# High and low columns side by side, and 512-column products in the first, q, k, v and widening stages

## What is computed

```python
h = rms_norm(x, attn_norm_g)
q, k, v, p = split(h @ w_in)            # 4 x 1024 columns
q, k = rms_norm(heads(q)), rms_norm(heads(k))
a = moba_attention(q, k, v, rel_bias)   # 8 heads of 128, one block of 256 keys, causal
m = multiscale_pool(p, pool_w, pool_scale)
x = x + concat(a, m) @ w_out            # "mix"
x = x + conv_ffn(rms_norm(x), w_up, conv_w, conv_b, w_down)   # "up" to 2 x 5632, "down"
```

## Time and profile before

| what | value |
|---|---|
| median of 3 runs | 2434.01 us (2433.1 to 2434.31) |
| the profiled execution | 2437.58 us |
| its span, first to last instruction | 2435.8 us |
| PE matmul busy | 2407.7 us, 99% |
| VectorE, ScalarE, GpSimd busy | 73%, 48%, 24% |
| mean granted TensorE clock | 0.998 |

### The profile page before, as it was taken

How to read it: one execution, slowest core, us unless ns; L and a number is a source line. 1 busy time by engine, 2 the same in 40 slices (tenths; PEclk the granted TensorE clock), 3 DMA queues, 4 the chain that set the end, 5 groups by cost and what they waited for, 6 DMA issues and landing times.

```text
span 2435.8 us, 53642 instructions
## 1 busy us (share of the span) xinstructions
PE 2407.7 (99%) x18808; PEld 2321.6 (95%) x18808; DVE 1769.6 (73%) x3095; ACT 1162.7 (48%) x1647; POOL 578.4 (24%) x402
## 2 busy tenths in 40 slices
PE   8999999999999999999999999999999999999998
PEld 8999899999999988898999999999999999999987
DVE  6877877777777755578888878888882566666665
ACT  5444444444444444447566643333544444444443
POOL 0400000000000000005242447777777300100100
PEclk9999999999999999999999999999999999999999
DMA  7554555555555666666555555555555555555544
GB/s 272 193 172 145 187 185 187 177 188 189 181 186 185 207 186 189 186 216 198 179 169 172 170 166 177 172 175 194 171 175 173 184 168 163 162 164 175 157 162 140
DMA packets 152398, 438.21 MB, mean 180 GB/s; under 512 B 32324, under 2 KB 47213, under 8 KB 152189
## 3 DMA queue, kind: packets, MB, share of 16 engines
q1 hardware_dynamic: 148844, 424.68, 53.5%
q0 software_dynamic: 3184, 12.14, 1.8%
q10 hardware_dynamic: 288, 0.30, 0.0%
HBM read 434.88 MB, written 11.09 MB: 183 GB/s over the span
## 4 chain that ended last, share of the span: by engine, by line
PE 95%; DVE 2%; DMA 1%; ACT 1%; issue 1%; DVEq 0%; SPq 0%; POOL 0%; ACTq 0%
PE bank L1121 24%; PE bank L1122 24%; PE bank L1123 24%; PE bank L1115 11%; PE bank L1116 6%; PE bank L1355 1%; DVE wlo L1569 1%; PE bank L1475 1%; PE bank L1326 1%; PE bank L1465 1%; PE bank L1455 1%; PE bank L1118 0%; DMA raw<-w_qkv 0%; PE bank L1482 0%; ACT whi L627 0%
## 5 line engine op out<-in xcount | busy, mean ns | idle before, releaser
L1121 PE MATMUL bank<-xhl,whi 128*128 128x256 f32 (+1 forms) x4494 | 1285.6, 286 | 4.9 <-DVE wlo L1569 3.9
L1123 PE MATMUL bank<-xhl,wlo 128*128 128x256 f32 (+1 forms) x4494 | 1278.3, 284 | 0.0
L1122 PE MATMUL bank<-xhl,whi 128*128 128x256 f32 (+1 forms) x4494 | 1277.6, 284 | 0.0
L627 ACT CAST whi<-raw 128x1024 fp32r<-128x1024 f32 x784 | 810.8, 1044 | 574.5 <-PE bank L1123 431.5
L1569 DVE TENSOR_TENSOR wlo<-raw,whi 128x1024 fp32r<-128x1024 f32 x624 | 765.8, 1238 | 263.4 <-ACT whi L627 259.2
L1121 PEld LDWEIGHTS bank<-xhl,whi 128*128 128x128 f32 x4494 | 849.8, 189 | 8.0 <-DVE wlo L1569 4.2
L1123 PEld LDWEIGHTS bank<-xhl,wlo 128*128 128x128 f32 x4494 | 848.9, 189 | 0.0
L1122 PEld LDWEIGHTS bank<-xhl,whi 128*128 128x128 f32 x4494 | 845.5, 188 | 0.8 <-issue 0.2
L568 POOL TENSOR_TENSOR wlo<-raw,whi 128x1024 fp32r<-128x1024 f32 x160 | 379.2, 2378 | 128.0 <-ACT whi L627 128.0
L1115 PE MATMUL bank<-fhl,whi 128*128 128x512 f32 x928 | 329.1, 398 | 0.0
L1116 PE MATMUL bank<-fhl,wlo 128*128 128x256 f32 x960 | 264.3, 281 | 0.0
(11 more groups left out here) (283 smaller groups left out, 2436.5 us busy)
## 6 DMA issues: line engine op xcount, KB each, us to landing
raw<-w_up SPq DMA_DIRECT2D x176, 512.0 KB, 3.9
raw<-w_na SPq DMA_DIRECT2D x128, 512.0 KB, 3.7
raw<-w_ssm SPq DMA_DIRECT2D x96, 512.0 KB, 3.9
raw<-w_glu SPq DMA_DIRECT2D x96, 512.0 KB, 3.5
raw<-w_down SPq DMA_DIRECT2D x80, 512.0 KB, 3.8
raw<-w_qkv SPq DMA_DIRECT2D x48, 512.0 KB, 3.8
raw<-w_mix SPq DMA_DIRECT2D x32, 512.0 KB, 3.7
raw<-w_outa SPq DMA_DIRECT2D x32, 512.0 KB, 3.6
```

Of the source, the lines that this page charges most:

```text
L627: A.copy(whi[s][:, :], raw[s][:, :]).then_inc(sem("hi_done"), 1)
L1121: T.matmul(to_, wh, xh_, start=head, stop=False)
L1122: T.matmul(to_, wh, xl_, start=False, stop=False)
L1123: ins = T.matmul(to_, wl, xh_, start=False, stop=last)
```

## The change

**Layout.** `xh` and `xl` share one row of 544 columns for each K-tile (`XW`), `fh`/`fl` and `oh`/`ol` rows of 512: the 256 high columns that a product reads end where the 256 low ones begin. **Products.** pin, qkv and up join the stages with two matmuls for a K-tile, and in all of these the 512 columns are now one run. **Evacuation.** In pin, qkv and up, ScalarE first copies the bank's upper half to `lows` (an area of `sq`), then VectorE adds it to the lower half and multiplies by the norm, in two dependent instructions instead of one. **Order.** In `up` the third split is moved ahead of the first taps on VectorE, and the gate and the tap on ScalarE behind casts.

```diff
+        XW = 2 * TOK
+        xh, xl = xhl[:, 0:KT * XW], xhl[:, TOK:KT * XW]
...
+        fh, fl = fhl[:, 0:2 * FT * SEQ], fhl[:, SEQ:2 * FT * SEQ]
...
+        lows = sq[:, 0:SEQ]
...
+            def lower(phase, i, j, k):
+
+                wait_chunk_done(act, phase, i, j)
+                act.wait_ge(sem("bank_free"), tile(phase, i, k) + 2)
+                A.copy(lows[:, :], pbank(phase, k)[:, SEQ:2 * SEQ]).then_inc(sem("low_out"), 1)
...
             def qkv(i, before=True, pooled=False):
                 for j in range(12):
                     split("qkv", i, j)
                     m, jj = divmod(j, 6)
                     attn = before or m
+                    if jj % 2:
+                        lower("qkv", i, j, j // 2)
                     if jj == 2 and attn:
                         probs(i * 2 + m)
...
+                split("up", i, 1)
+                if lead:
+                    act.wait_ge(sem("acc_done"), 2 + 32)
+                lower("up", i, 1, 0)
+                split("up", i, 2)
+                tap(0)
+                split("up", i, 3)
...
+                gate(nt[:, 0:SEQ], cg[:, :], ACT.Silu, "eg_up")
+                lower("up", i, 3, 1)
+                tap(1)
...
-                    if wide and phase in ("mix", "down", "naout"):
-                        both = pb_[:, 0:2 * n].rearrange("p (t n) -> p t n", t=2)
+                    if wide and phase in ("pin", "qkv", "mix", "up", "down", "naout"):
                         if not last:
-                            T.matmul(both, wh, halves(mh, ml, o, n), start=head, stop=False)
+                            T.matmul(pb_[:, 0:2 * n], wh, mh[:, o:o + 2 * n], start=head, stop=False)
                         ins = T.matmul(out, wl, mh[:, o:o + n], start=False, stop=False)
...
+            def scaled_halves(phase, i, k, out, r):
+
+                dve.wait_ge(sem("low_out"), low_tile(phase, i, k) + 1)
+                ch.link(V.tensor_tensor(out, pbank(phase, k)[:, 0:SEQ], lows[:, :], ADD))
+                freed(phase, i, k, V.tensor_tensor(out, out, r, MUL))
...
                 split("up", i, 1)
-                scaled("up", i, 1, 0, ug[:, 2:SEQ + 2], rs[1], SEQ, META)
+                scaled_halves("up", i, 0, ug[:, 2:SEQ + 2], rs[1][:, META:TOK])
+                split("up", i, 2)
                 taps(ug, cg, 0, i).then_inc(sem("cg_ready"), 1)
-                split("up", i, 2)
                 split("up", i, 3)
-                scaled("up", i, 3, 1, uv[:, 2:SEQ + 2], rs[1], SEQ, META)
+                scaled_halves("up", i, 1, uv[:, 2:SEQ + 2], rs[1][:, META:TOK])
```

More of the change, by code:

```diff
@@ L155, in program @@
         cv = at("cv", SEQ, F32, U + 3136)
[L157 to L158 removed]
+        a = Y + 2 * 16 * SEQ * 4
+        b = a + 28 * SEQ * 4
         praw = at("praw", 8 * TOK, F32, a)
@@ L270, in tile, with low_tile @@
             return i * PHASES[phase][2] + (first(phase, 2) + k)
+        def low_tile(phase, i, k):
+            return tile(phase, i, k) - (16 if phase == "up" else 0)
         def pbank(phase, k):
@@ L766, in qkv @@
                         pool_hi(2 * m + jj // 4)
+            lower_pin(0)
+            lower_pin(1)
             split("pin", 1, 2)
+            lower_pin(2)
             split("pin", 1, 3)
-            with act.Fori(2, 4) as i:
+            lower_pin(3)
+            for i in range(2, 4):
                 for j in range(4):
                     split("pin", i, j)
+                    if j % 2:
+                        lower_pin(2 * i + j // 2)
             ch.begin()
@@ L805, in up, with tap @@
             def up(i, lead=0, last=False):
[L806 to L820 removed]
+                def tap(k):
+                    u, c = ((ug, cg), (uv, cv))[k]
+                    evacuated("up", i, k)
+                    A.activation(c[:, :], u[:, 0:SEQ], ACT.Identity,
+                                 bias=vcol("ffn_conv", 4 * k + 3, i, 8),
+                                 scale=vcol("ffn_conv", 4 * k, i, 8)).then_inc(sem("tap_done"), 1)
+                if not lead:
+                    split("up", i, 0)
+                split("up", i, 1)
[5 more added lines that the diff above has]
+                split("up", i, 3)
+                if last:
+                    split("down", 0, 0)
+                act.wait_ge(sem("cg_ready"), i + 1)
+                gate(nt[:, 0:SEQ], cg[:, :], ACT.Silu, "eg_up")
+                lower("up", i, 3, 1)
+                tap(1)
             up(0, 1)
@@ L1243, in mixing @@
             def mixing(n, part, kts, out=None, start=False, stop=False, done=True):
-                product("mix", part, n, n % 2, fh, fl, kts, SEQ, 0, SEQ, start, stop, out, done)
+                product("mix", part, n, n % 2, fh, fl, kts, 2 * SEQ, 0, SEQ, start, stop, out, done)
             pe.wait_ge(sem("pool_free"), 4)
@@ L1508, in projecting @@
             def projecting(n, n_tile, kts, start=False, stop=False, done=True):
-                product("naout", n // 4, n % 4, n_tile % 2, oh, ol, kts, SEQ, 0, SEQ, start, stop,
+                product("naout", n // 4, n % 4, n_tile % 2, oh, ol, kts, 2 * SEQ, 0, SEQ, start, stop,
                         {2: bank[2], 3: bank[3]}.get(n_tile), done)
@@ L1696, in _ @@
             pin(7)
+            ch.end()
             def softmax_in(h):
```

96 lines of the change are left out of this document (39 added, 57 removed).

## The result

The changed kernel takes 2447.43 us (median; 2447.05 to 2449.04), the kernel before 2434.01: a ratio of 1.0056 with a 95% interval from 1.0044 to 1.0068. It is 13.4 us slower, where 2 us less were forecast. (One of the five executions of the kernel before took 8751 us and stands apart; without it their median is 2433.6.) The profiled execution took 2447.05 us, its span is 2445.3 us and its mean granted clock 0.998, as before.

What follows compares the result with a forecast made beforehand. PE was taken to bound the kernel: -12.0 (mix, down, naout), -4 (up), 0 (pin), +11 (q, k, v) and +3 (first head) sum to -2 us, so 2434.0 becomes 2432 us; 8-in-10 range 2416 to 2452.

Steps and rivals of the forecast that it cites:

- Bound: Whole kernel: PE work is 95% of the last chain, so time is gained by PE's rate and lost where PE waits.
- Products, the gain: Mix, down, naout: one 512-column run takes 225.0 ns, a K-tile 343.3 instead of 353.3; -12.0 us over 1200 K-tiles.
- Up: Widening product: VectorE bounds the loop at 11.27 us against PE's 11.36; 4 us gained, from -9 to +5.
- PE without idle time in up: Sign in the profile after: PE was to idle 0.3 us an iteration in up; no idle time would prove the working wrong.
- Pin: First product: 128 K-tiles could give 1.5 us, but late weights and eight more VectorE instructions; 0 booked, from -1.5 to +1.
- q, k, v and the first head: Heads: PE stalls before `pts` and the squares, +11 us; extra steps and GpSimd contention in the first head, +3 us.
- One run is no cheaper than two: Rival: the 512-column product keeps 235 ns, the 12.0 us gain is gone, stalls stay; 2446 us, chance 0.27.
- One run is cheaper still: Rival: 512 columns take 216 ns, mix, down and naout gain 11 us more; 2421 us, chance 0.20.
- the 3.6 us between that execution and the median: Forecast's base: the median lies 3.6 us below the profiled 2437.6 us, so the sum was applied to 2434.0.

Runs made afterwards that it cites:

- run 512: Not a follow-up kernel: a matmul's 512 moving columns read as one adjacent run, in the changed kernel against two runs of 256 before; 235.4 ns.
- inner_64: up_apart with a 64-byte gap behind the rows of x, so the rows of mix, down and naout start 64 bytes further; 2424.9 us.
- up_apart: Kernel before with only up in the two-matmul form, 512 columns as two runs of 256 on the old rows; 2426.6 us, ratio 0.9969.
- up_alone: Changed kernel with pin and q, k, v back to three 256-column matmuls and one VectorE step, new rows kept; 2431.4 us.
- layout_alone: Kernel before on the new side-by-side rows, products and evacuations as before, na reading its low rows 64 bytes early; 2439.5 us.
- windows_late: Changed kernel with GpSimd's window sums held back by a semaphore wait until the second pair of heads has its first query; 2449.0 us.
- low_64: up_apart with the low rows of x, and all behind them in SBUF, 64 bytes further from the high rows; 2435.1 us.
- low_256: up_apart with the low rows of x, and all behind them in SBUF, 256 bytes further from the high rows; 2427.0 us.
- layout_full: layout_alone with na's 256-column products reading their own low rows where they belong; 2441.1 us.
- two_runs: Changed kernel with the 512-column matmuls naming the same adjacent columns as two runs of 256; 2448.0 us.
- all_apart: inner_64 with pin and q, k, v also in two-run 512-column form on old rows, two-step joins, ScalarE and VectorE reordered; 2427.2 us.

## Why the prediction was wrong

**Bound.** Right: PE's rate and PE's waits set the time.

**Products, the gain: the step that failed.** I read 353.3 - 343.3 = 10.0 ns out of down's K-tile as the price of two runs and booked -12.0 us. It measured 0: mix, down and naout took 0.1 us less together, and 512 columns in one run took 235.4 ns, where I took 225.0 and gave 235.0 as the upper end. The error was to fit a fixed price from 256 and 272 columns and to give the rest to the one feature that the change removes. Two things that I had in hand spoke against it. The 272-column matmuls read in runs of four columns and had the same 11.7 ns above their columns as one run of 256; and the earlier trace rows has the same two-run instructions at 346.7 ns. The form could not be what makes 353.3, since down has both levels, tile by tile, before and after. What makes them is not found: moving the rows by 64 bytes (inner_64) gave 348.9 in half the tiles.

**Up.** -4 forecast, -8.5 measured, inside the -9 to +5. VectorE's steps were 0.12 us shorter than I took from 517.53 - 516.96, so PE bounds the loop, at 348.8 ns a K-tile. That is slower than the 343.3 I had for PE, and at 11.16 us a loop faster than the 11.27 I had for VectorE. I had named PE without idle time in up as a sign that the working was wrong, and so it was.

**Pin.** 0 forecast. Its last K-tile starts at 56.8 us, in up_apart, up_alone and layout_alone at 57.3, 56.8 and 57.7: no difference that stands out.

**q, k, v and the first head.** +14 forecast, +15.5 measured. Mechanism and size hold for the later heads: 1.6 us instead of 1.9 in each, 0.84 us of PE idle before `pts` for the 1.1 forecast and 0.48 before the squares for 0.8. The first two heads cost 6.2 where 3 was booked for the first, with 1 to 6 as its bounds; in windows_late, where GpSimd's sums are held back, all 6.2 are gone. About 1.6 of the 6.2 are the 3.4 us at the lower clock, which the sum did not have. The Trainium skill (SBUF — State Buffer, "Who interferes with whom") says that a VectorE instruction with two SBUF inputs contends with a GpSimd instruction that reads SBUF. The trace agrees: the new multiplication takes 2.52 us and ends 0.3 us behind GpSimd's instruction of 3.61.

**What the sum did not contain.** +7 us from the rows of x in products that the diff does not name. I had looked at the new layout as a means for one matmul and not asked what else reads it: the 272-column stages and na, 2576 K-tiles with about 3 ns each. No rival had it. low_64, low_256 and layout_full show the loss and its source.

**The rivals.** "One run is no cheaper than two" came out with its 235 ns, and its 2446 us is close to 2447.4, but by luck in part: it had up 6.5 us too slow and the 7 us of the rows not at all. "One run is cheaper still" is out, by the same 235.4 ns. The Trainium skill (TensorE: Matmul & The Clock Gate, "Wait — 56ns, not 53.3ns?") has N / 2.4 GHz + about 2.5 ns for a warm matmul, which makes an estimate of 215.8 ns for 512 columns; the measured 235.4 for this type of product decides against it. The 2447.4 us lie inside the range of 2416 to 2452; the direction and the cause of the forecast do not hold.

**The yardstick.** The profiled execution of before began mix at 225.6 us; the nine experiments whose front has its instructions (three of them on the new rows) began it at 220.4 to 222.8. I had taken the 3.6 us between that execution and the median for an offset of the whole. The trace shows a late start instead: the cast of a weight chunk of q, k, v waited 6.98 us for its transfer, in up_apart 3.69; GpSimd's first sum started at 63.23 us instead of 59.97 and the first sum of squares at 74.79 instead of 71.66. The slow clock behind it goes with another 1.2 us in the second head. That the other executions of before had none of this is likely from their times, but no trace of them shows it.

## What to carry to other kernels

Before moving an operand for the sake of one instruction, list every other instruction that reads it, and cost them at the new addresses. A residue that a fit leaves over belongs to no cause until a row shows it with and without; the trace may have a counterexample in the same stage. When an edit changes nothing, look whether it reached the chip: the recorded source pattern of two_runs tells that it did not. A copy that waits for a chunk's end must not stand ahead of one that PE needs at that moment.

## What the runs showed of the hardware

- The rate of these matmuls depends on where the moving rows start, by shifts of 64 bytes: 375.0 or 378.3 ns for a K-tile of 272 columns, 349 or 353 for 768 columns in up. For 272 columns, at a spacing of 1088 bytes, a low row 17408, 17536 or 17664 bytes from its high row (multiples of 128) gave the faster value and one 17472 away the slower; at a spacing of 2176 bytes only 1088 was run, 64 more than a multiple of 128, and it was slow. For other forms no single rule held.
- The same instructions on the same rows run at more than one level: 346.7 or 353.3 ns a K-tile in down, constant over an output tile. 64 bytes of shift made it 348.9 and 353.3 in turn. What picks the level was not found.
- Two runs of 256 columns far apart cost what one of 512 costs, with the rows elsewhere too: 247.85 us for down in before and after.
- A VectorE instruction that reads two operands in SBUF can be held by GpSimd: the multiplication took 2.52 us for 0.43, a split 3.77 in a later head, where 1.22 is usual. With GpSimd's sum cut in eight no split took over 1.6 us.
- After a wait of 1.85 us in the first head the granted clock was 0.50 for 3.4 us and a K-tile took 640 ns; after 1.9 us in all_apart it stayed at 1.00.
